# Feed-forward entry by column half, tile 0's weights split sooner, tile 1 in one region; a key chunk through another buffer; orders around keys and values

## The chip, the cores and the metric

The kernel runs on one core of a Trainium2 chip. The metric is the device time of one execution in microseconds (us), the median of several runs. All times inside the execution are from one profiled execution of the kernel before, counted from the start of its span.

## What is computed

A decoder trunk of two layers on 256 tokens of width 1024, all in float32:

```python
# layer 0: x += NSA(RMSNorm(x));      x += ConvGLU(RMSNorm(x))
# then:    k, v = RMSNorm_kv(x) @ kv_w                 # shared keys and values
# layer 1: x += DiffAttn(RMSNorm(x)); x += ConvGLU(RMSNorm(x))
# out = RMSNorm(x)
def conv_glu_ffn(h, w_in, conv_w, conv_b, w_out):
    u = h @ w_in                                       # 1024 -> 2 * 2752
    up = jnp.pad(u, ((0, 0), (CONV_WIDTH - 1, 0), (0, 0)))
    c = conv_b
    for tap in range(CONV_WIDTH):                      # 3 taps over the tokens
        c = c + up[:, tap:tap + S] * conv_w[tap]
    gate, val = c[..., :FFN_DIM], c[..., FFN_DIM:]
    return (jax.nn.silu(gate) * val) @ w_out
```

## The kernel before

Every float32 operand of a matmul is split into a high part (rounded, `..._hi`) and a low part (the rest, `..._lo`), and a product is three matmuls: high by high, high by low, low by high. The weights come in as chunks of 128 x 2048. SyncE loads a chunk into `stage` (two slots), ScalarE writes its high part into `win_hi` in two halves of 1024 columns, VectorE subtracts and writes `win_lo`, and TensorE uses both. SyncE issues loads in one fixed order, each after the wait that frees its slot; the code of each engine is likewise an order written out by hand, and an engine stands still until its next instruction's semaphores are there. Nothing is reordered between VectorE instructions or between ScalarE instructions.

The stages in order: six projection groups of the sparse attention (chunks 0 to 11; chunk 8 is the first half of the keys), compression and attention, the output projection (4 chunks, `C_WO`), the feed-forward of layer 0 (`ffn(0, ...)`), keys, values and queries of the differential attention (12 chunks from `C_KV`), its attention, its output projection (`C_DO`), `ffn(1, ...)`, the last norm.

A feed-forward runs over 22 tiles of 128 gate and 128 value columns. Tile j is `up(j)` on TensorE (into `psU`), then on VectorE and ScalarE a scaling by the row of 1/rms, a 3-tap convolution, SiLU, product and split (`act_hi`, `act_lo`), then `down(j)` on TensorE into `psA`. TensorE runs up(j+1) ahead of down(j). `up` uses one matmul over 512 columns (high weights by the high and low activations side by side) and one over 256; its two halves lie in two column regions of a bank, which ScalarE's copy (`u_part`) and a VectorE add bring together. Tile 0 is special: `up_raw` uses activations that are transposed unscaled while the norm is still being computed, and the scaling comes later through a row made by `row_T` and a VectorE copy (L1699).

Around the start of a feed-forward: `add_y` adds the projection to `x` in four pieces (token tile t, column half h) as TensorE finishes them; `raw_T` transposes a piece of x; `raw_hi` (ScalarE) and `raw_lo` (VectorE) write the transposed activations' parts; `square_halves`, `root_of`, `first_mean` and `newton_a` to `newton_d` make 1/rms; `split_in(j, b, h)` splits half h of the input weights of tile j, `split_out` the output weights of a tile. `step(j, b)` is one tile's work on ScalarE or VectorE.

## Time and profile before

| | |
|---|---|
| three runs | 663.27, 663.92, 664.14 us; median 663.92 |
| the profiled execution | 662.02 us, of which its span is 660.2 us |
| granted TensorE clock | 0.997 of full speed |
| TensorE matmuls (PE) busy | 632.3 us (96% of the span) |
| VectorE (DVE) busy | 535.2 us (81%) |
| ScalarE (ACT) busy | 417.7 us (63%) |

Busy shares are means over very different stages. In the timeline views below a row is: start in us, length in us, engine, line of the code, operation, output <- inputs, shapes, count; in brackets the idle time of the engine just before it and what ended it. Matmuls overlap in the pipeline, so a matmul's length is more than its spacing.

### The profile page before, as it was taken

The numbers are of one execution on the slowest core, as the hardware profiler recorded it, in microseconds if no ns is written. First come the engines' busy times: TensorE is split into PE (matmuls) and PEld (weight loads), VectorE is DVE, ScalarE is ACT, GpSimd is POOL, SyncE is SP. The second block draws the span as 40 slices with busy tenths as digits, with TensorE's granted clock in tenths as the row PEclk, the third lists the DMA queues.
The fourth block names the chain that finished last, engine by engine and source line by source line (L and its number), as shares of the span: only waits on it lengthen the run. The fifth ranks groups of instructions, "written<-read, shape, count | busy, mean of one in ns | idle before, by whom it ended". The sixth has DMA issues, their size and how long they took to land.

```text
span 660.2 us, 10782 instructions
## 1 busy us (share of the span) xinstructions
PE 632.3 (96%) x3614; PEld 527.9 (80%) x3614; DVE 535.2 (81%) x987; ACT 417.7 (63%) x815; POOL 25.2 (4%) x70
## 2 busy tenths in 40 slices
PE   8999989999999999999999999979999999999995
PEld 7998756678878888888888788757878888888894
DVE  4587598956998888888988547796899888888996
ACT  7554377827766666666667454673966666666665
POOL 2100000000000000000004000060000000000000
PEclk9999999999999999999999999999999999999998
DMA  8685030126455555545525545305455555555521
GB/s 287 239 283 210 5 123 2 66 72 248 159 196 213 195 190 187 198 186 191 186 77 192 189 147 184 120 1 216 169 178 215 189 189 186 189 190 184 191 105 65
DMA packets 21441, 109.12 MB, mean 165 GB/s; under 512 B 2592, under 2 KB 2976, under 8 KB 12448
## 3 DMA queue, kind: packets, MB, share of 16 engines
q1 hardware_dynamic: 21120, 108.48, 45.9%
q8 instruction: 19, 0.31, 0.2%
q10 hardware_dynamic: 288, 0.22, 0.1%
q14 instruction: 14, 0.11, 0.1%
HBM read 107.64 MB, written 1.05 MB: 165 GB/s over the span
## 4 chain that ended last, share of the span: by engine, by line
PE 76%; DVE 14%; ACT 4%; POOL 3%; issue 2%; DMA 1%; DVEq 0%; ACTq 0%; POOLq 0%
PE psU L545 19%; PE psA L406 12%; PE psA L408 12%; PE psA L407 12%; PE psU L550 10%; DVE win_lo L1531 2%; DVE stat L1803 2%; DVE win_lo L1445 2%; DVE arena L1832 1%; DVE arena L1559 1%; PE psU L758 1%; PE psU L743 1%; PE psU L525 1%; PE psU L524 1%; PE psU L523 1%
## 5 line engine op out<-in xcount | busy, mean ns | idle before, releaser
L545 PE MATMUL psU<-hA,win_hi 128*128 128x512 f32 x608 | 190.7, 395 | 1.0 <-DVE win_lo L1531 1.0
L550 PEld LDWEIGHTS psU<-hA,win_lo 128*128 128x128 f32 x608 | 114.2, 188 | 26.6
L550 PE MATMUL psU<-hA,win_lo 128*128 128x256 f32 x608 | 119.4, 278 | 0.0
L1531 DVE TENSOR_TENSOR win_lo<-stage,win_hi 128x1024 fp32r<-128x1024 f32 x89 | 108.6, 1222 | 5.7 <-ACT win_hi L1095 5.6
L1095 ACT ACTIVATE win_hi<-stage 128x1024 fp32r<-128x1024 f32 x92 | 96.0, 1050 | 9.1 <-PE psA L408 5.6
L545 PEld LDWEIGHTS psU<-hA,win_hi 128*128 128x128 f32 x608 | 95.3, 189 | 4.2 <-ACT win_hi L1095 1.4
L1445 DVE TENSOR_TENSOR win_lo<-stage,win_hi 128x1024 fp32r<-128x1024 f32 (+3 forms) x59 | 65.9, 1154 | 21.0 <-ACT win_hi L1032 20.7
L1559 DVE SCALAR_TENSOR_TENSOR arena<-arena,prm 128x255 f32<-128x255 f32 (+1 forms) x168 | 77.3, 481 | 3.7 <-ACT arena L1107 0.7
L406 PE MATMUL psA<-wout_hi,act_hi 128*128 128x512 f32 x176 | 69.3, 394 | 2.8 <-DVE act_lo L1598 2.2
L407 PE MATMUL psA<-wout_lo,act_hi 128*128 128x512 f32 x176 | 68.7, 390 | 0.0
L408 PE MATMUL psA<-wout_hi,act_lo 128*128 128x512 f32 x176 | 68.5, 389 | 0.0
L1032 ACT ACTIVATE win_hi<-stage 128x1024 fp32r<-128x1024 f32 (+3 forms) x56 | 53.5, 1002 | 21.6 <-PE psA L408 15.7
L1107 ACT ACTIVATE arena<-arena,prm 128x256 f32<-128x256 f32 x84 | 46.0, 595 | 26.0 <-DVE arena L1580 21.8
L406 PE MATMUL psA<-win_hi,hA 128*128 128x512 f32 (+3 forms) x160 | 60.3, 377 | 1.3 <-DVE win_lo L1445 0.8
L408 PE MATMUL psA<-win_hi,hA 128*128 128x512 f32 (+3 forms) x160 | 59.3, 371 | 0.0
L407 PE MATMUL psA<-win_lo,hA 128*128 128x512 f32 (+3 forms) x160 | 59.2, 370 | 0.0
L1549 DVE TENSOR_TENSOR wout_lo<-stage_out,wout_hi 128x1024 fp32r<-128x1024 f32 x42 | 51.3, 1222 | 0.0
L1116 ACT ACTIVATE arena<-psU 128x512 f32<-128x512 f32 x38 | 22.7, 598 | 44.3 <-PE psU L550 44.2
L1573 DVE TENSOR_TENSOR arena<-psU,arena 128x512 f32<-128x512 f32 x38 | 26.3, 692 | 22.5 <-ACT arena L1116 22.5
L1103 ACT ACTIVATE wout_hi<-stage_out 128x1024 fp32r<-128x1024 f32 x42 | 44.0, 1047 | 0.0
L1263 ACT ACTIVATE arena<-psA,stat 128x128 f32<-128x128 f32 (+1 forms) x88 | 35.9, 429 | 7.9 <-DVE stat L1803 7.6
L406 PEld LDWEIGHTS psA<-wout_hi,act_hi 128*128 128x128 f32 x176 | 33.0, 188 | 9.5 <-DVE act_lo L1598 2.6
(250 smaller groups left out, 1058.5 us busy)
## 6 DMA issues: line engine op xcount, KB each, us to landing
stage<-in_w_ffn_in SPq DMA_DIRECT2D x44, 1024.0 KB, 5.5
stage_out<-in_w_ffn_out SPq DMA_DIRECT2D x44, 516.0 KB, 3.5
stage<-in_w_kv SPq DMA_DIRECT2D x8, 1024.0 KB, 5.0
stage<-in_w_group SPq DMA_DIRECT2D x5, 1024.0 KB, 5.3
stage<-in_w_nsa_out SPq DMA_DIRECT2D x4, 1024.0 KB, 4.8
stage<-in_w_dq SPq DMA_DIRECT2D x4, 1024.0 KB, 4.9
stage<-in_w_dout SPq DMA_DIRECT2D x4, 1024.0 KB, 4.8
stage<-in_w_phi SPq DMA_DIRECT2D x2, 1024.0 KB, 4.8
```

Of the source, the lines that this page charges most:

```text
L406: mm(out, xh, wh, start=start, stop=False)
L407: mm(out, xh, wl, start=False, stop=False)
L408: return mm(out, xl, wh, start=False, stop=stop)
L545: mm(o, win_hi[:, slot, cs], hA[:, k, :, :].rearrange("p a q -> p (a q)"), start=k == 0, stop=False)
L550: last = mm(o[:, 0:S], win_lo[:, slot, cs], hA_hi[:, k2, :], start=False, stop=k2 == KT - 1)
L1032: act.activation(win_hi[:, s % 2, cs], stage[:, n % 2, cs], ACT.Copy).then_inc(sem["in_hi"], 1)
L1095: act.activation(win_hi[:, slot, h * W // 2:(h + 1) * W // 2], stage[:, slot, h * W // 2:(h + 1) * W // 2], ACT.Copy).then_inc(sem["in_hi" ...
L1107: act.activation(conv[:, b, g, :], src, ACT.Identity, bias=prm[:, b, 4 * g + 3:4 * g + 4], scale=prm[:, b, 4 * g + 2:4 * g + 3]).then_inc( ...
L1445: last = dve.tensor_tensor(win_lo[:, s % 2, cs], stage[:, n % 2, cs], win_hi[:, s % 2, cs].bitcast(F32), sub)
L1531: last = dve.tensor_tensor(win_lo[:, slot, cs], stage[:, slot, cs], win_hi[:, slot, cs].bitcast(F32), sub)
L1549: dve.tensor_tensor(wout_lo[:, b, :], stage_out[:, b, 0:D], wout_hi[:, b, :].bitcast(F32), sub).then_inc(sem["out_lo"], 1)
L1559: dve.scalar_tensor_tensor(conv[:, b, g, k:S], u_sum[:, g, 0:S - k], prm[:, b, 4 * g + 2 - k:4 * g + 3 - k], conv[:, b, g, k:S], ALU.mult, ...
```

## The change

It does the following.

- **Key chunk.** Chunk 8 is loaded into `keysT` (unused by then) right behind chunk 6, and not into `stage`; chunk 10 then waits only for chunk 6's slot, and some `phi` pieces are loaded at other places.
- **Feed-forward entry, by column half.** The last chunk of the output projection (`out_last`) now finishes column half 0 of both token tiles and then column half 1; `raw_T`, `add_y` and the squares follow that order, and only two column-half-1 transposes remain behind the projection.
- **Tile 0's weights.** Half 0 of tile 0's input weights is split into slot 1 of `wout_hi` and `wout_lo`, which needs no free slot of `win_hi`. `split_out(0, 0)` moves ahead of it on ScalarE and VectorE. `split_in(1, 1, 0)` moves forward between the activations' parts; the Newton steps come behind all of `raw_lo`.
- **Tile 1 in one region.** `up_second` uses three matmuls over 256 columns; ScalarE's `u_part` copy and VectorE's add fall away. On ScalarE both conv_first instructions now come ahead of `split_in(3, 1, 0)`; on both engines `split_in(3, 1, 1)` moves behind `act_hi` and `act_lo`.
- **Last tile.** ScalarE does SiLU, then the first half of the output weights, then `act_hi`, then the second half.
- **Keys and values.** `raw_T(2, 1, 0)` moves into `down_last`, `raw_T(2, 1, 1)` behind the first two k of the projection; VectorE adds piece (1, 1) behind the first two `h_lo`; the split of chunk `C_KV + 3` moves ahead of the wait for 1/rms.

```diff
+                if s != C_EARLY:
+                    load_main(s, a_groups[s // 2][s % 2], w4)
+                if s == C_EARLY - 2:
+                    sp.dma_start(keysT[:, :], a_groups[C_EARLY // 2][0]).then_inc(sem["keys_in"], 16)
                 if s == 2:
                     sp.dma_start(cols[:, O_PE:NCOL], a_cols[:, O_PE:NCOL]).then_inc(sem["params_in"], 16)
                     sp.dma_start(cmask[:, :], a_mask).then_inc(sem["mask_in"], 16)
-                if 3 <= s < 11:
-
-                    i = s - 3
+                for i in PHI_PIECES.get(s, ()):
...
+                            if half == 0:
+                                raw_T(2, 1, 1)
...
+                for n in range(2):
+                    for t in range(TT):
+                        if n == 1:
+                            raw_T(n_norm, t, 0)
+                        for k in range(2):
+                            last = out_three(h_hi, h_lo, slot, t, n, k, 6 + k)
+                        if n + t < 2:
+                            last.then_inc(sem["y_ready"], 1)
+                last.then_inc(sem["in_used"], 1)
+
+            def out_part(s0, h_hi, h_lo, h_waits, per_chunk, c, t, ks):
 
                 pe_.wait_ge(sem["oT_hi"], h_waits + per_chunk * (c + 1))
...
+                    pe_.wait_ge(sem["w0_half"], layer + 1)
                     for i, k in enumerate(T_ORDER):
+                        if i < 4:
+                            w_hi, w_lo = wout_hi[:, 1, :], wout_lo[:, 1, :]
+                        else:
+                            w_hi, w_lo = (w[:, slot, W // 2:W] for w in (win_hi, win_lo))
+                        if i == 4:
+                            pe_.wait_ge(sem["in_hi"], 2 * (first + 1))
+                            pe_.wait_ge(sem["in_lo"], first + 1)
                         if i == 2:
                             raw_T(n, 1, 1)
 
...
-                            last = up_pairs(g, 1, slot, range(kh * KT // 2, (kh + 1) * KT // 2))
+                            for k in range(kh * KT // 2, (kh + 1) * KT // 2):
+                                cs = slice(k * 2 * P + g * P, k * 2 * P + g * P + P)
+                                last = three_w((psT, psO)[g][:, 1, 0:S], slot, cs, k, k == 0, k == KT - 1)
...
                         if i == 2 and layer == 0:
                             raw_T(2, 0, 0)
+                            raw_T(2, 1, 0)
...
-                    split_in(j + 2, b, 1)
+                    if not late:
+                        split_in(j + 2, b, 1)
                     act.wait_ge(sem["prod"], j + (f0 + 1))
                     if not (isinstance(j, int) and j + f0 < 2):
 
                         act.wait_ge(sem["out_used"], j + (f0 - 1))
                     act.activation(act_hi[:, b, :], prod[:, b, :], ACT.Copy).then_inc(sem["a_hi"], 1)
+                    if late:
+                        split_in(j + 2, b, 1)
...
-                        act.activation(wout_hi[:, 1, cs], stage_out[:, 1, cs], ACT.Copy).then_inc(sem[done], 1)
-                    act.wait_ge(sem["gate2"], f0 + NJ)
-                    act.activation(silu[0:LAST, 1, :], conv[0:LAST, 1, 0, :], ACT.Silu).then_inc(sem["silu"], 1)
+                    act.activation(wout_hi[:, 1, HALVES[0]], stage_out[:, 1, HALVES[0]], ACT.Copy).then_inc(sem["last_hi"], 1)
                     act.wait_ge(sem["prod"], f0 + NJ)
                     act.activation(act_hi[0:LAST, 1, :], prod[0:LAST, 1, :], ACT.Copy).then_inc(sem["a_hi"], 1)
+                    act.activation(wout_hi[:, 1, HALVES[1]], stage_out[:, 1, HALVES[1]], ACT.Copy).then_inc(sem["out_hi"], 1)
...
+                split_out(0, 0, layer > 0)
                 split_in(0, 0, 0)
                 split_in(0, 0, 1)
-                split_out(0, 0, layer > 0)
                 inst, waits = (1, KT) if layer == 0 else (3, 4 * KT)
                 if layer == 0:
                     act.wait_ge(sem["eps_ready"], 1)
                 act.activation(warm, eps, ACT.Sqrt)
-                square_halves(n, 0)
-                root_of(n, 0)
+                for t in range(TT):
+                    square_half(n, t, 0)
                 raw_hi(layer, inst, waits, 0)
                 raw_hi(layer, inst, waits, 2)
-                square_halves(n, 1)
+                split_in(1, 1, 0)
+                square_half(n, 0, 1)
                 raw_hi(layer, inst, waits, 4)
-                root_of(n, 1)
+                square_half(n, 1, 1)
                 raw_hi(layer, inst, waits, 6)
-                split_in(1, 1, 0)
+                for t in range(TT):
+                    root_of(n, t)
                 split_in(1, 1, 1)
 
                 act.activation(warm, eps, ACT.Silu)
                 step(0, 0, halves=False)
-                step(1, 1)
+                step(1, 1, halves=False, late=True)
...
                 g = c // 2
                 if c == 1:
+                    split(C_KV + 3)
                     act.wait_ge(sem["rstd"], 2)
...
-                def step(j, b):
-                    add_and_scale(j, b)
+                def step(j, b, lo_first=False):
+                    if lo_first:
+                        times_row(j, psU[:, b, :, 0:S])
+                        take_params(j + 1, 1 - b)
+                    else:
+                        add_and_scale(j, b)
                     split_in(j + 2, b, 0)
                     taps(j, b)
                     product(j, b)
+                    if lo_first:
+                        product_lo(j, b)
                     split_in(j + 2, b, 1)
-                    product_lo(j, b)
+                    if not lo_first:
+                        product_lo(j, b)
                     split_out(j + 1, 1 - b)
...
+                take_params(0, 0)
+                split_out(0, 0)
                 split_in(0, 0, 0)
                 add_y(n, 0, 0, "in_used", first)
+                add_y(n, 1, 0, "in_used", first)
+                split_in(0, 0, 1)
                 add_y(n, 0, 1, "in_used", first)
-                split_in(0, 0, 1)
-                add_y(n, 1, 0, "in_used", first)
-                first_mean(n, 0)
-                add_y(n, 1, 1, "in_used", first)
+                for t in range(TT):
+                    first_mean(n, t)
                 raw_lo(0)
                 raw_lo(1)
+                add_y(n, 1, 1, "in_used", first)
                 raw_lo(2)
                 raw_lo(3)
-                first_mean(n, 1)
-                take_params(0, 0)
-                split_out(0, 0)
+                split_in(1, 1, 0)
                 raw_lo(4)
+                raw_lo(5)
+                raw_lo(6)
+                raw_lo(7)
                 newton_a()
-                raw_lo(5)
                 newton_b()
-                raw_lo(6)
                 newton_c()
-                raw_lo(7)
                 newton_d()
                 rows_of_rstd()
-                split_in(1, 1, 0)
...
-            for h in range(2):
-                for t in range(TT):
-                    add_y(2, t, h, "out_used", NJ)
+            add_y(2, 0, 0, "out_used", NJ)
+            add_y(2, 1, 0, "out_used", NJ)
+            add_y(2, 0, 1, "out_used", NJ)
             h_lo(hA_lo, hA_hi, O_KG, range(2))
+            add_y(2, 1, 1, "out_used", NJ)
             split(C_KV, (1,))
             h_lo(hA_lo, hA_hi, O_KG, range(2, KT))
```

Tile 1 on VectorE in a feed-forward, from its first instruction after `split_out(1, 1)` (`arena` holds the convolution's buffers; L1559 or L1618 are the taps, L1593 or L1652 the product). Before:

```order
L1573 TENSOR_TENSOR arena<-psU,arena 128x512 [waits u_part]
L1554 COPY prm<-stage_out 128x8 [waits stage_out0_full]
L1580 TENSOR_TENSOR arena<-arena 128x512 [waits u_sum]
L1531 TENSOR_TENSOR win_lo<-stage,win_hi 128x1024 [waits in_hi]
L1559 SCALAR_TENSOR_TENSOR arena<-arena,prm 128x255 [waits conv0]
L1559 SCALAR_TENSOR_TENSOR arena<-arena,prm 128x254 [waits gate1]
L1559 SCALAR_TENSOR_TENSOR arena<-arena,prm 128x255 [waits conv0]
L1559 SCALAR_TENSOR_TENSOR arena<-arena,prm 128x254 [waits val1]
L1593 TENSOR_TENSOR arena<-arena 128x256 [waits val2,silu]
L1531 TENSOR_TENSOR win_lo<-stage,win_hi 128x1024 [waits in_hi]
L1598 TENSOR_TENSOR act_lo<-arena,act_hi 128x256 [waits a_hi]
L1549 TENSOR_TENSOR wout_lo<-stage_out,wout_hi 128x1024 [waits out_hi]
```

and now:

```order
L1627 TENSOR_TENSOR arena<-psU,arena 128x512 [waits in_used]
L1613 COPY prm<-stage_out 128x8 [waits stage_out0_full]
L1590 TENSOR_TENSOR win_lo<-stage,win_hi 128x1024 [waits in_hi]
L1618 SCALAR_TENSOR_TENSOR arena<-arena,prm 128x255 [waits conv0]
L1618 SCALAR_TENSOR_TENSOR arena<-arena,prm 128x254 [waits gate1]
L1618 SCALAR_TENSOR_TENSOR arena<-arena,prm 128x255 [waits conv0]
L1618 SCALAR_TENSOR_TENSOR arena<-arena,prm 128x254 [waits val1]
L1652 TENSOR_TENSOR arena<-arena 128x256 [waits val2,silu]
L1657 TENSOR_TENSOR act_lo<-arena,act_hi 128x256 [waits a_hi]
L1590 TENSOR_TENSOR win_lo<-stage,win_hi 128x1024 [waits in_hi]
L1608 TENSOR_TENSOR wout_lo<-stage_out,wout_hi 128x1024 [waits out_hi]
```

The add and the wait for `u_part` are gone, and the second `win_lo` split stands behind `act_lo`. The first `win_lo` split stands where it stood, ahead of the taps.

The same tile on ScalarE, from `split_out(1, 1)` on (L1107 or L1157 are the two conv_first, L1124 or L1174 is SiLU). Before:

```order
L1103 ACTIVATE wout_hi<-stage_out 128x1024 [waits stage_out1_full]
L1116 ACTIVATE arena<-psU 128x512 [waits in_used,prod,conv_params]
L1095 ACTIVATE win_hi<-stage 128x1024 [waits in_used,stage1_full]
L1107 ACTIVATE arena<-arena,prm 128x256 [waits u_norm]
L1107 ACTIVATE arena<-arena,prm 128x256
L1124 ACTIVATE arena<-arena 128x256 [waits gate2]
L1095 ACTIVATE win_hi<-stage 128x1024
L1130 ACTIVATE act_hi<-arena 128x256 [waits prod]
L1103 ACTIVATE wout_hi<-stage_out 128x1024 [waits out_used,stage_out0_full]
```

and now:

```order
L1153 ACTIVATE wout_hi<-stage_out 128x1024 [waits stage_out1_full]
L1157 ACTIVATE arena<-arena,prm 128x256 [waits in_used,u_norm,prod,conv_params]
L1157 ACTIVATE arena<-arena,prm 128x256
L1145 ACTIVATE win_hi<-stage 128x1024 [waits in_used,stage1_full]
L1174 ACTIVATE arena<-arena 128x256 [waits gate2]
L1181 ACTIVATE act_hi<-arena 128x256 [waits prod]
L1145 ACTIVATE win_hi<-stage 128x1024
L1153 ACTIVATE wout_hi<-stage_out 128x1024 [waits out_used,stage_out0_full]
```

The copy from `psU` is gone, the first `win_hi` copy has moved from ahead of the two conv_first to behind them, and the second from ahead of `act_hi` to behind it.

TensorE at the end of layer 0's feed-forward and the start of keys and values (`psU<-ident,x` are the transposes of `raw_T`). Before:

```order
L417 MATMUL psU<-ident,x 128x128 [waits x_new]
L417 MATMUL psU<-ident,x 128x128 x3
L406 MATMUL psA<-wout_hi,act_hi 128x512
L407 MATMUL psA<-wout_lo,act_hi 128x512
L408 MATMUL psA<-wout_hi,act_lo 128x512
L417 MATMUL psU<-ident,x 128x128 [waits x_new]
L417 MATMUL psU<-ident,x 128x128 x3
L417 MATMUL psU<-ident,x 128x128 [waits x_new]
L417 MATMUL psU<-ident,x 128x128 x3
L417 MATMUL psU<-ident,x 128x128 [waits x_new]
L417 MATMUL psU<-ident,x 128x128 x3
L406 MATMUL psA<-win_hi,hA 128x512 [waits xT_hi,xT_lo,kv_half,in_hi]
```

and now:

```order
L430 MATMUL psU<-ident,x 128x128 [waits x_new]
L430 MATMUL psU<-ident,x 128x128 x3
L430 MATMUL psU<-ident,x 128x128 [waits x_new]
L430 MATMUL psU<-ident,x 128x128 x3
L419 MATMUL psA<-wout_hi,act_hi 128x512
L420 MATMUL psA<-wout_lo,act_hi 128x512
L421 MATMUL psA<-wout_hi,act_lo 128x512
L430 MATMUL psU<-ident,x 128x128 [waits x_new]
L430 MATMUL psU<-ident,x 128x128 x3
L419 MATMUL psA<-win_hi,hA 128x512 [waits xT_hi,xT_lo,kv_half,in_hi]
```

Two of the four pieces are transposed ahead of the last `down`, one behind it, and the fourth not before the projection's first two k.

## Rows read from the trace of the kernel before

**Rows 1.** Timeline of TensorE (PE): its waits, and starts named.

```profile
45.07 0.33 PE L408 MATMUL psA<-win_hi,hA 128*128 128x368 f32 x1
...
45.55 0.47 PE L406 MATMUL psA<-win_hi,hA 128*128 128x512 f32 x1
...
160.30 0.60 PE L417 MATMUL psU<-ident,x 128*128 128x128 f32 x4
...
161.34 0.36 PE L507 MATMUL psA<-hA,win_hi 128*128 128x256 f32 x1 [0.44 <-ACT hA L1072]
...
168.51 0.70 PE L545 MATMUL psU<-hA,win_hi 128*128 128x512 f32 x2 [0.51 <-DVE win_lo L1531]
...
183.73 0.50 PE L406 MATMUL psA<-wout_hi,act_hi 128*128 128x512 f32 x1 [1.10 <-DVE act_lo L1598]
...
192.15 0.40 PE L406 MATMUL psA<-wout_hi,act_hi 128*128 128x512 f32 x1
...
342.11 0.50 PE L406 MATMUL psA<-wout_hi,act_hi 128*128 128x512 f32 x1 [0.28 <-DVE act_lo L1668]
...
347.57 0.47 PE L406 MATMUL psA<-win_hi,hA 128*128 128x512 f32 x1 [0.32 <-DVE hA L1468]
...
364.74 0.47 PE L406 MATMUL psA<-win_hi,hA 128*128 128x512 f32 x1 [0.58 <-DVE win_lo L1445]
...
491.53 0.50 PE L406 MATMUL psA<-wout_hi,act_hi 128*128 128x512 f32 x1 [1.12 <-DVE act_lo L1598]
```

**Rows 2.** Timeline of VectorE (DVE), layer 0, tiles 0 to 2.

```profile
168.29 0.42 DVE L1699 COPY arena<-psA 128x256 f32<-128x256 f32 x1
...
177.22 0.69 DVE L1573 TENSOR_TENSOR arena<-psU,arena 128x512 f32<-128x512 f32 x1
...
178.55 1.22 DVE L1531 TENSOR_TENSOR win_lo<-stage,win_hi 128x1024 fp32r<-128x1024 f32 x1
...
181.70 0.43 DVE L1593 TENSOR_TENSOR arena<-arena 128x256 f32<-128x256 f32 x1
...
183.26 0.42 DVE L1598 TENSOR_TENSOR act_lo<-arena,act_hi 128x256 fp32r<-128x256 f32 x1
...
184.73 0.68 DVE L1573 TENSOR_TENSOR arena<-psU,arena 128x512 f32<-128x512 f32 x1
...
190.77 0.42 DVE L1598 TENSOR_TENSOR act_lo<-arena,act_hi 128x256 fp32r<-128x256 f32 x1
```

**Rows 3.** Timeline of ScalarE (ACT), layer 0, tiles 0 and 1.

```profile
168.07 1.28 ACT L1184 ACT_TABLE_LOAD   x1
...
178.67 1.10 ACT L1107 ACTIVATE arena<-arena,prm 128x256 f32<-128x256 f32 x2 [0.80 <-DVE arena L1580]
...
181.04 1.04 ACT L1095 ACTIVATE win_hi<-stage 128x1024 fp32r<-128x1024 f32 x1
...
182.16 0.42 ACT L1130 ACTIVATE act_hi<-arena 128x256 fp32r<-128x256 f32 x1
```

**Rows 4.** Timeline of SyncE's queue: issue of tile 0's output weights, both layers.

```profile
147.11 0.43 SPq L369 DMA_DIRECT2D stage_out<-in_w_ffn_out  x1
...
455.23 0.43 SPq L369 DMA_DIRECT2D stage_out<-in_w_ffn_out  x1
```

**Rows 5.** DMA issues of those two moments; last: us from issue to landing.

```profile
stage_out<-in_w_ffn_out SPq DMA_DIRECT2D x1, 516.0 KB, 5.7
...
stage_out<-in_w_ffn_out SPq DMA_DIRECT2D x1, 516.0 KB, 5.8
```

**Rows 6.** Timeline of ScalarE, last tile of layer 0 and keys' start.

```profile
339.21 1.16 ACT L1154 ACTIVATE wout_hi<-stage_out 128x512 fp32r<-128x512 f32 x2 [1.04 <-PE psA L408]
...
346.07 3.03 ACT L1042 ACTIVATE hA<-psU,cols 128x256 fp32r<-128x256 f32 x8 [0.70 <-PE psU L417]
```

**Rows 7.** Timeline of VectorE, keys and values.

```profile
346.94 0.88 DVE L1468 SCALAR_TENSOR_TENSOR hA<-psU,cols,hA 128x256 fp32r<-128x256 f32 x2 [0.40 <-ACT hA L1042]
...
351.21 2.35 DVE L1445 TENSOR_TENSOR win_lo<-stage,win_hi 128x1024 fp32r<-128x1024 f32 x2
```

More of the change, by code:

```diff
@@ L54, in sum_place @@
 def sum_place(n, t, h):
-    return 2 * h + t if n == 2 else 2 * t + h
+    return 2 * h + t if n in (1, 2, 3) else 2 * t + h
 T_ORDER = (0, 2, 1, 3, 4, 6, 5, 7)
@@ L612, in ffn @@
                 down(1, 1, False)
-                pe_.wait_ge(sem["u_sum"], sums(1))
+                pe_.wait_ge(sem["u_norm"], f0 + layer + 2)
                 up(3, 1)
@@ L1029, in split @@
                 for h in halves:
-                    act.wait_ge(stage_full[n % 2], 16 * (n // 2 + 1))
+                    if s == C_EARLY:
+                        act.wait_ge(sem["keys_in"], 16)
+                    else:
+                        act.wait_ge(stage_full[n % 2], 16 * loads_of(n))
                     cs = slice(h * w // 2, (h + 1) * w // 2)
-                    act.activation(win_hi[:, s % 2, cs], stage[:, n % 2, cs], ACT.Copy).then_inc(sem["in_hi"], 1)
+                    act.activation(win_hi[:, s % 2, cs], (keysT if s == C_EARLY else stage[:, n % 2, :])[:, cs], ACT.Copy).then_inc(sem["in_hi"], 1)
             def h_hi(dst, off, inst, lo_done=0, ks=range(KT)):
@@ L1091, in split_in @@
                     slot = (first + b) % 2
+                    if isinstance(j, int) and j == 0 and h == 0:
+                        act.wait_ge(stage_full[slot], 16 * loads_of(stage_of(first)))
+                        act.activation(wout_hi[:, 1, :], stage[:, slot, 0:W // 2], ACT.Copy).then_inc(sem["in_hi"], 1)
+                        return
+                    if isinstance(j, int) and j == 0:
+                        act.wait_ge(sem["in_used"], first - 1)
                     if h == 0:
-                        act.wait_ge(stage_full[slot], 8 * j + (16 * (stage_of(first + b) // 2 + 1) - 8 * b))
+                        act.wait_ge(stage_full[slot], 8 * j + (16 * loads_of(stage_of(first + b)) - 8 * b))
                         act.wait_ge(sem["in_used"], j + (first - 1))
@@ L1108, in conv_first, with step @@
                                    bias=prm[:, b, 4 * g + 3:4 * g + 4], scale=prm[:, b, 4 * g + 2:4 * g + 3]).then_inc(sem["conv0"], 1)
-                def step(j, b, halves=True):
+                def step(j, b, halves=True, late=False):
                     act.wait_ge(sem["conv_params"], j + (f0 + 1))
@@ L1378, in _ @@
                         exps(u, u, "d", free_diff, psU[:, u, :, :])
-                if c < 11:
+                if c < 11 and c != 1:
                     split(C_KV + c + 2)
@@ L1419, in _ @@
             for t in range(TT):
-                square_halves(4, t)
+                for h in range(2):
+                    square_half(4, t, h)
                 root_of(4, t)
@@ L1709, in ffn @@
                 split_out(1, 1)
-                step(1, 1)
+                step(1, 1, lo_first=True)
                 with dve.Fori(1, NJ // 2 - 1) as i:
@@ L1935, in _ @@
                 g = c // 2
+                if c == 1:
+                    split(C_KV + 3)
                 if c % 2:
```

86 lines of the change are left out of this document (48 added, 38 removed).

## The prediction

> **What bounds the kernel now.** I read the shares first (the table ahead of the rows): TensorE is busy 96% of the span, so only the places count where it stands still, and what stands behind them. The timeline of TensorE gives these [rows 1]. In layer 0: 0.44 us at 161.34 (`up_raw` waits for the first activation part), 0.51 at 168.51 (`up_second` waits for tile 1's low weights), 1.10 at 183.73 (`down(1, 1)` waits for `act_lo`), 0.28 at 342.11 (last tile), 0.32 at 347.57 and 0.58 at 364.74 (keys and values). The matmul at 45.55 starts 0.15 after the end of that at 45.07. A refill of the pipeline comes on top of each: a matmul of 512 columns follows another after 0.23 us although it is 0.39 long, so an idle time stands for 0.16 to 0.18 more; I add that. Layer 1 repeats layer 0 with a shift of 307.8 us (491.53 less 183.73). Everything that the change could win so is 0.33 + 0.45 x 2 + 0.76 + about 1, and 2 x 2.6 at the feed-forwards: some 8 us.
>
> The second look, at VectorE through tiles 0 to 2 [rows 2], decides how much of the 2.6 is to be had. From the row copy at 168.29 to the last `act_lo` at 190.77 VectorE has almost no pause. Tile 2's `act_lo` starts at 190.77 and TensorE can follow 0.47 later (as 183.26 is followed by 183.73 [rows 1, 2]), at 191.24; it really takes `down(2, 0)` at 192.15 [rows 1]. VectorE has thus only 0.91 us in hand there, and whatever TensorE wins before must fit into that or into time that VectorE wins.
>
> **Feed-forward, tile 1: VectorE's time.** Before, tile 1 takes VectorE from 177.22 to 184.73, 7.51 us [rows 2]. Now, with S as its start:
> - The multiply reads `psU` directly. ScalarE's first conv_first starts 0.73 behind it (before: 1.45 behind the add's start, the second of two such operations [rows 2, 3]). The two take 1.10, and only then comes ScalarE's copy of 1.04 for `split_in(3, 1, 0)` [rows 3]. VectorE's low half can start at S + 2.8 (pipelined starts overlap by some 0.1). Before it started at S + 1.33 (178.55) without a wait. The add that falls away saves 0.6 of VectorE's work, but VectorE now waits 2.1.
> - From this half to the product it is 3.15 (178.55 to 181.70) as before: product at S + 5.95. `act_hi` follows after 0.46 (181.70 to 182.16): S + 6.4. `act_lo` starts at S + 6.85.
> - ScalarE's copy of the upper half now starts behind `act_hi`, so VectorE's comes at S + 7.85, and with this half and `split_out`, 1.22 each less the overlap, tile 2 starts at S + 10.1. Before, all of it from `act_lo` on took 1.47 (183.26 to 184.73).
>
> Tile 1 costs VectorE 10.1 in place of 7.5: +2.6. Then tile 2 runs as before, 6.04 to its `act_lo` (184.73 to 190.77).
>
> **Feed-forward, ahead of tile 1.** The chain from the row copy to S is the same list of instructions, so S moves by as much as the row copy does. Replayed with the durations of these rows: the output projection ends at 160.30 [rows 1]; the chunk's column half 0 of token tile 0 is transposed 3.6 us earlier, at 156.7, if `add_y(0, 0)` is done. But VectorE now does `split_out(0, 0)` and half a weight split ahead of that add, and the output weights land only at 147.11 + 5.7 = 152.8 [rows 4, 5]. Copy on ScalarE, two VectorE splits of 1.14 and the add bring x to 156.9: 0.25 late, so the projection ends at 160.55. `up_raw` starts 0.35 later, not 1.04 later as before, takes 6.25 as before and ends at 167.15. Its Newton steps are done just before (last `raw_lo` at 165.6, then some 1.1). The row copy comes at 167.55 in place of 168.29: 0.75 earlier. In layer 1 the weights land at 455.23 + 5.8, which is 0.4 later against the rest; the gain there is 0.35.
>
> So `down(2, 0)` can start at 191.24 + 2.6 - 0.75 = 193.1 against 192.15: **layer 0 loses 0.9, layer 1 loses 1.3**. The waits of 0.44 and 0.51 go and that of 1.10 does too in name, but `down(1, 1)` waits some 2.2 (its `act_lo` at S + 6.85 with S = 176.5 is where it was, while TensorE is 1 us early), and `down(2, 0)` waits near 1. Tile 3 has room again (0.7 in hand), and from there on TensorE binds; nothing is given back. TensorE's own cost of one region is hidden there: 48 matmuls in place of 32, 0.1 us in all if 256 columns follow at 0.12; were it a full 1 us (a far bound), it would lie in the 2.2.
>
> A table load stands on this chain: ScalarE's load for SiLU at 168.07 takes 1.28 [rows 3]; in the new order it ends near 167.9, and tile 0's multiply is done at 168.6, so it is hidden. The Trainium skill (ScalarE: Activation LUTs, Rules for kernel authors) says to budget about 2.7 us for a switch to another table set. By that figure, as an estimate, the load would end 0.6 us after the multiply and each layer would lose 0.6 more. The trace's 1.28 decides; the case stands with the rival that the row comes later, and adds less than 0.05 to its chance.
>
> **Last tile (each layer).** ScalarE copies both halves of the output weights from 339.21 for 1.16 ahead of SiLU [rows 6]. Now SiLU goes first and its product is some 1.0 earlier; `act_lo` would be ready at 341.2, before TensorE gets there at 341.66. The wait at 342.11 goes: -0.45 in each layer (bounds 0 and -0.45).
>
> **Keys and values.** Two adds bring x to TensorE at 344.0 and 344.6; transposes and the last `down` end at 346.1. ScalarE's copies start 0.42 after the second transposes, VectorE's part 0.87 after that (346.07 to 346.94) and TensorE 0.63 later (347.57) [rows 1, 6, 7]: 346.55, 1.0 earlier. But the fourth transposes come 2.7 later, at 349.3, and cost their 0.46 there. ScalarE's copies 4 to 7 of 3.03 / 8 each wait for them, VectorE's behind these, and so the split of chunk `C_KV + 1`, at 351.21 before [rows 7], starts at 352.2; its half is there at 353.5. TensorE wants it at 352.5. The second half of group 0 starts at 353.5 against 347.57 + 5.44 = 353.0. So far +0.5 (with the last tile's 0.45 in it). The squares slip by 2.3 us and with them 1/rms, but the split of `C_KV + 3` no longer waits for it, so the 0.58 + 0.18 at 364.74 go. Together with the last tile of layer 0: **-0.3** (bounds +0.5, if the stall stays, and -1.2, if the fourth transposes are early enough).
>
> **Key chunk.** The start at 45.55 [rows 1] is behind a load; now the chunk is there early. **-0.3** (bounds: +0.4, if a megabyte in the queue makes chunk 7 late, which I find 0.5 us in time, and -0.33).
>
> **The sum**: +0.9 + 1.3 - 0.3 (last tile of layer 0, keys and values) - 0.45 (last tile of layer 1) - 0.3 = **+1.15 us**. The profiled execution is 662.02 with a span of 660.2; I expect 661.3 and 663.2. The median of before lies 1.9 above its profiled execution, so the same step gives 665.1.
>
> **Rivals.**
> - *The wait for ScalarE's split is not felt* (faster). If tile 1's lower half is ready when VectorE asks for it, tile 1 costs 7.5 - 0.6 + 1.1 = 8.0 and `down(2, 0)` starts as TensorE gets there, 2.0 and 1.6 earlier: -3.6 - 1.1 = -4.7, 659.2. For it: 2 us of waits vanish at sight. Against: the order puts both conv_first ahead of the copy. It decides from a wait of under 1 us there. Half-way cases give 661 to 663. Chance 0.2 together.
> - *The row comes later* (slower). Newton's steps now stand behind every activation part; if they end 0.8 late, they reach past the end of `up_raw` by 0.5 (they have 0.3 in hand) and each layer loses 0.5 more: 666.1. The same follows if the table load of 1.28 ends 1.3 later than I put it. Chance 0.2. The table switch by the Trainium skill's figure would act in this way and give 666.3.
> - *Keys and values stay as they are, or the key chunk makes chunk 7 late*: 1 us worse, 666. Chance 0.1.
> - The forecast, 663.9 to 665.9: chance 0.5.
>
> Under 0.2% (1.3 us) a measurement of this kernel tells nothing from no change. The forecast lies within it for the most part, its upper third and the two slow rivals beyond. Faster 0.2, same 0.42, slower 0.38. The range takes in all but the whole gain and the sum of all losses: 661.8 to 667.0.
>
> **What the new profile would show.** Right: VectorE idle about 2 us before `win_lo` L1590 in tile 1, released by ScalarE's L1145, and 0.6 more behind `act_lo`; TensorE waiting 2 us and more at `down(1, 1)` and near 1 at `down(2, 0)` for `act_lo`; no wait at the row, nor at the last tile; a new wait of 1 us in the first projection group for `C_KV + 1`. The prediction is wrong if `down(2, 0)` has no wait, or if `up_raw` ends after 168 against the same start.

## The result and the profile after

| | before | changed kernel |
|---|---|---|
| median of 15 runs each, on one chip | 662.93 us (662.22 to 664.79) | 665.98 us (664.33 to 668.57) |
| ratio | | 1.0045, 95% interval 1.0032 to 1.0058 |
| profiled execution | 662.02, span 660.2 | 664.87, span 663.1 |
| TensorE busy | 632.3 us | 634.3 us |
| VectorE, ScalarE busy | 535.2, 417.7 us | 534.6, 415.6 us |

The changed kernel is 0.45% slower, 3.0 us by the medians and 2.9 by the profiled executions. The forecast was 1.15 us slower, 665.1 us, with a range from 661.8 to 667.0.

The timeline of VectorE after, layer 0, tile 1 and the start of tile 2 (start us, duration us, engine, line, operation, tiles, shapes; in brackets the idle time before it and who ended it). It answers to [rows 2]:

```profile
176.69 0.68 DVE L1627 TENSOR_TENSOR arena<-psU,arena 128x512 f32<-128x512 f32 x1
177.29 0.17 DVE L1613 COPY prm<-stage_out 128x8 f32<-128x8 f32 x1
179.57 1.23 DVE L1590 TENSOR_TENSOR win_lo<-stage,win_hi 128x1024 fp32r<-128x1024 f32 x1 [2.12 <-ACT win_hi L1145]
180.71 1.91 DVE L1618 SCALAR_TENSOR_TENSOR arena<-arena,prm 128x255 f32<-128x255 f32 x4
182.73 0.43 DVE L1652 TENSOR_TENSOR arena<-arena 128x256 f32<-128x256 f32 x1
183.63 0.43 DVE L1657 TENSOR_TENSOR act_lo<-arena,act_hi 128x256 fp32r<-128x256 f32 x1 [0.48 <-ACT act_hi L1181]
184.58 1.23 DVE L1590 TENSOR_TENSOR win_lo<-stage,win_hi 128x1024 fp32r<-128x1024 f32 x1 [0.52 <-ACT win_hi L1145]
185.72 1.22 DVE L1608 TENSOR_TENSOR wout_lo<-stage_out,wout_hi 128x1024 fp32r<-128x1024 f32 x1
186.86 0.69 DVE L1632 TENSOR_TENSOR arena<-psU,arena 128x512 f32<-128x512 f32 x1
```

Tile 1 lasts from 176.69 to 186.86, 10.17 us against 7.51. The 2.12 at 179.57 is the wait for ScalarE's lower copy; on ScalarE that copy stands behind both first convolution steps:

```profile
177.49 1.09 ACT L1157 ACTIVATE arena<-arena,prm 128x256 f32<-128x256 f32 x2 [3.63 <-DVE prm L1613]
178.49 1.05 ACT L1145 ACTIVATE win_hi<-stage 128x1024 fp32r<-128x1024 f32 x1
```

ScalarE had nothing to do for 3.63 us ahead of those steps. The timeline of TensorE after, which answers to [rows 1]: `down(1, 1)` and `down(2, 0)` of layer 0, the keys and values, and the same two places in layer 1:

```profile
184.12 0.50 PE L419 MATMUL psA<-wout_hi,act_hi 128*128 128x512 f32 x1 [2.12 <-DVE act_lo L1657]
184.46 0.40 PE L420 MATMUL psA<-wout_lo,act_hi 128*128 128x512 f32 x1
...
193.37 0.50 PE L419 MATMUL psA<-wout_hi,act_hi 128*128 128x512 f32 x1 [0.64 <-DVE act_lo L1657]
...
347.89 0.47 PE L419 MATMUL psA<-win_hi,hA 128*128 128x512 f32 x1 [0.19 <-DVE hA L1524]
...
354.90 0.47 PE L419 MATMUL psA<-win_hi,hA 128*128 128x512 f32 x1 [0.84 <-issue]
...
493.36 0.78 PE L419 MATMUL psA<-wout_hi,act_hi 128*128 128x512 f32 x1 [2.12 <-DVE act_lo L1657]
493.93 0.63 PE L420 MATMUL psA<-wout_lo,act_hi 128*128 128x512 f32 x1
494.36 0.63 PE L421 MATMUL psA<-wout_hi,act_lo 128*128 128x512 f32 x1
...
503.36 0.40 PE L419 MATMUL psA<-wout_hi,act_hi 128*128 128x512 f32 x1
```

Both layers wait 2.12 us at `down(1, 1)`. In layer 0 the matmuls behind it go on as before (0.34 from the first to the second). In layer 1 they take 0.63 and follow each other after 0.43 instead of 0.23 us. The view by stretches shows why (PEclk is the third number from the end: the granted clock, 1.00 for 2.4 GHz and 0.50 for 1.2 GHz):

```profile
492.00:496.00 4.00, 2.64 (x6) 2.16 (x7) 3.00 (x4) 3.57 (x5) 0.00 (x0) 0.68 0.00 0
496.00:500.00 4.00, 4.00 (x20) 3.37 (x19) 3.93 (x9) 1.67 (x5) 0.00 (x0) 0.90 0.64 224
```

The clock was halved for 3.4 us behind that wait (0.32 and 0.10 of 4 us are missing, and half clock lacks half: 1.68 times 2). Before, this place shows 1.00 throughout.

The starts of like matmuls give the time section by section, in us (the profiled executions; "phi" is the first matmul with `phi_k`, "projection" the first matmul that reads `hB_hi`, "last down" the first matmul of the last `down` of the loop, "end of keys and values" the first matmul behind the sixteen transposes of `tokA`; the numbers are differences of such starts, so a line that only moved shows nothing):

| section | before | changed | change |
|---|---|---|---|
| start to first matmul of group 0 | 8.29 | 8.95 | +0.66 |
| to phi | 63.70 | 63.16 | -0.54 |
| to output projection | 59.13 | 59.11 | -0.02 |
| layer 0: projection to down(0, 0) | 43.04 | 42.20 | -0.84 |
| to down(1, 1) | 9.57 | 10.70 | +1.13 |
| to down(2, 0) | 8.42 | 9.25 | +0.83 |
| to last down | 144.05 | 144.20 | +0.15 |
| to the end of keys and values | 52.20 | 51.91 | -0.29 |
| to layer 1's projection | 54.83 | 54.86 | +0.03 |
| layer 1: projection to down(0, 0) | 38.73 | 38.33 | -0.40 |
| to down(1, 1) | 9.57 | 10.69 | +1.12 |
| to down(2, 0) | 8.42 | 10.00 | +1.58 |
| to the end | 160.3 | 159.7 | -0.5 |

### The profile page after: what moved, and what is told of

It is laid out like the page before. It is cut to its first block, busy times and chain, and to the rows that moved or that the text cites. A ratio compares the mean times of both kernels' runs of the same rounds, so it can differ in the third digit from the quotient of the medians.

```text
span 663.1 us, 10832 instructions
## 1 busy us (share of the span) xinstructions
PE 634.3 (96%) x3646; PEld 531.6 (80%) x3646; DVE 534.6 (81%) x985; ACT 415.6 (63%) x813; POOL 23.6 (4%) x70
## 4 chain that ended last, share of the span: by engine, by line
PE 75%; DVE 15%; ACT 3%; DMA 2%; issue 2%; POOL 2%; SPq 0%; DVEq 0%; ACTq 0%; POOLq 0%
PE psU L588 18%; PE psA L419 12%; PE psA L420 12%; PE psA L421 12%; PE psU L593 9%; DVE win_lo L1590 2%; DMA stage_out<-in_w_ffn_out 2%; DVE stat L1869 2%; DVE win_lo L1501 2%; DVE arena L1618 1%; DVE arena L1898 1%; PE psU L430 1%; PE psU L802 1%; PE psU L787 1%; DVE wout_lo L1608 1%
## 5 line engine op out<-in xcount | busy, mean ns | idle before, releaser
L588 PE MATMUL psU<-hA,win_hi 128*128 128x512 f32 x576 | 180.5, 395 | 0.0
L593 PEld LDWEIGHTS psU<-hA,win_lo 128*128 128x128 f32 x576 | 108.2, 188 | 25.2
L593 PE MATMUL psU<-hA,win_lo 128*128 128x256 f32 x576 | 113.1, 278 | 0.0
L1590 DVE TENSOR_TENSOR win_lo<-stage,win_hi 128x1024 fp32r<-128x1024 f32 x87 | 106.1, 1222 | 5.5 <-ACT win_hi L1145 5.5
L1145 ACT ACTIVATE win_hi<-stage 128x1024 fp32r<-128x1024 f32 x90 | 94.2, 1050 | 1.0 <-DMA stage<-in_w_ffn_in 1.0
L588 PEld LDWEIGHTS psU<-hA,win_hi 128*128 128x128 f32 x576 | 90.4, 189 | 2.8
L1501 DVE TENSOR_TENSOR win_lo<-stage,win_hi 128x1024 fp32r<-128x1024 f32 (+3 forms) x57 | 63.5, 1151 | 21.5 <-ACT win_hi L1077 21.4
L1618 DVE SCALAR_TENSOR_TENSOR arena<-arena,prm 128x255 f32<-128x255 f32 (+1 forms) x168 | 77.2, 480 | 3.7 <-ACT arena L1157 0.7
L1157 ACT ACTIVATE arena<-arena,prm 128x256 f32<-128x256 f32 x84 | 46.0, 595 | 33.8 <-DVE arena L1639 20.3
L1077 ACT ACTIVATE win_hi<-stage 128x1024 fp32r<-128x1024 f32 (+3 forms) x54 | 51.6, 1003 | 19.5 <-PE psA L421 15.8
L1632 DVE TENSOR_TENSOR arena<-psU,arena 128x512 f32<-128x512 f32 x36 | 24.9, 692 | 21.7 <-ACT arena L1166 21.7
L1174 ACT ACTIVATE arena<-arena 128x256 f32<-128x256 f32 x40 | 16.7, 418 | 38.7 <-DVE arena L1618 38.7
```

What stands on the lines that cost most here:

```text
L588: mm(o, win_hi[:, slot, cs], hA[:, k, :, :].rearrange("p a q -> p (a q)"), start=k == 0, stop=False)
L593: last = mm(o[:, 0:S], win_lo[:, slot, cs], hA_hi[:, k2, :], start=False, stop=k2 == KT - 1)
L1077: act.activation(win_hi[:, s % 2, cs], (keysT if s == C_EARLY else stage[:, n % 2, :])[:, cs], ACT.Copy).then_inc(sem["in_hi"], 1)
L1145: act.activation(win_hi[:, slot, h * W // 2:(h + 1) * W // 2], stage[:, slot, h * W // 2:(h + 1) * W // 2], ACT.Copy).then_inc(sem["in_hi" ...
L1157: act.activation(conv[:, b, g, :], src, ACT.Identity, bias=prm[:, b, 4 * g + 3:4 * g + 4], scale=prm[:, b, 4 * g + 2:4 * g + 3]).then_inc( ...
L1501: last = dve.tensor_tensor(win_lo[:, s % 2, cs], (keysT if s == C_EARLY else stage[:, n % 2, :])[:, cs], win_hi[:, s % 2, cs].bitcast(F32) ...
```

## The experiments

Runs e1 to e4 shared one chip (kernel before there: median 663.06), e5 to e8 another (662.69).

**e1: ScalarE's lower copy first.** In tile 1 the copy goes ahead of the wait for `u_norm`:

```diff
                     if halves:
                         act.activation(u_part, psU[:, b, :, S:2 * S], ACT.Copy).then_inc(sem["u_part"], 1)
-                        split_in(j + 2, b, 0)
+                    if halves or late:
                         split_in(j + 2, b, 0)
                     act.wait_ge(sem["u_norm"], j + (f0 + layer + 1))
                     for g in range(2):
                         conv_first(j, b, g, u_sum[:, g, :])
-                    if not halves:
+                    if not halves and not late:
                         split_in(j + 2, b, 0)
```

> The changed kernel, with one edit: in tile 1 ScalarE copies the lower half of tile 3's weights (split_in(3, 1, 0)) ahead of the two conv_first instead of behind them. My theory (the 2.1 us for which VectorE waits there set the time of both feed-forward heads): VectorE's wait of 2.12 us at 179.57 goes, down(1, 1) starts without a wait at 181.9 instead of 184.12, down(2, 0) near 191.2 instead of 193.37; in layer 1 the same 2.2 us, and with the wait of TensorE the stretch of half clock behind it, another 0.75. In all 4.5 to 5 us less than the changed kernel: a profiled execution near 660.0, 1.5 to 2 us faster than the kernel before. Rival (the chain is set by something else that is late next, so that the wait only moves): less than 1.5 us off the changed kernel, and a wait of 1 us or more still at down(1, 1).

Measured: median 660.52, ratio to before 0.9962 (0.9943 to 0.9982). The profiled execution took 662.74, not the 660.0 expected. Tile 1 in this kernel, ScalarE's lower copy and VectorE's timeline (3.1 us later as a whole, mainly because the clock was halved for 6.8 us at 98 to 106 us, in the attention):

```profile
178.32 1.07 ACT L1145 ACTIVATE win_hi<-stage 128x1024 fp32r<-128x1024 f32 x1 [1.35 <-DMA stage<-in_w_ffn_in]
179.79 0.69 DVE L1628 TENSOR_TENSOR arena<-psU,arena 128x512 f32<-128x512 f32 x1
180.39 0.16 DVE L1614 COPY prm<-stage_out 128x8 f32<-128x8 f32 x1
180.46 1.22 DVE L1591 TENSOR_TENSOR win_lo<-stage,win_hi 128x1024 fp32r<-128x1024 f32 x1
...
185.48 1.23 DVE L1591 TENSOR_TENSOR win_lo<-stage,win_hi 128x1024 fp32r<-128x1024 f32 x1 [0.53 <-ACT win_hi L1145]
```

ScalarE's copy itself waited 1.35 us for its load, and was done before VectorE needed it. The half follows without a wait, and TensorE goes from down(0, 0) to down(1, 1) in 8.47 us instead of 10.70, without a wait. To down(2, 0) it still takes 9.27, with a wait of 0.68:

```profile
185.00 0.50 PE L419 MATMUL psA<-wout_hi,act_hi 128*128 128x512 f32 x1
...
194.27 0.50 PE L419 MATMUL psA<-wout_hi,act_hi 128*128 128x512 f32 x1 [0.68 <-DVE act_lo L1658]
```

So one copy's place decides the sign of the whole change: from 0.45% slower to 0.4% faster. The rival (the wait only moves) is out: no wait is left at down(1, 1).

**e2: TensorE kept busy.** Ahead of `down(1, 1)`:

```diff
                 up(2, 0)
+                pe_.wait_ge(sem["u_norm"], f0 + layer + 2)
+                for k in range(8):
+                    mm(psT[:, 1, :], hA_hi[:, k % KT, 0:P], hA[:, k % KT, :, :].rearrange("p a q -> p (a q)"), start=True, stop=True)
                 down(1, 1, False)
```

> The changed kernel, with 8 more matmuls of 512 columns on TensorE ahead of down(1, 1) in each layer (1.85 us of work whose result nobody reads), so that TensorE waits 0.2 us there and not 2.1, and all else is where it was. My theory (a stretch of half clock follows when TensorE has stood still for 2.1 us, in some executions in one layer and in others in both, and this makes up 0.75 us and more of the loss and the wide spread of the changed kernel's times): no granted clock of 0.5 behind down(1, 1), the times lie close together near 664.2, 1 to 2 us under the changed kernel's median, although TensorE does more. Rival (the stretches of half clock come whatever TensorE did before): clock and spread as in the changed kernel, median the same or up to 0.3 us longer.

Measured: median 665.06, ratio 1.0033 (1.0018 to 1.0049). TensorE's wait is 0.26 and 0.29 us, and the clock stays at 1.00 behind it in both layers:

```profile
182.39 1.98 PE L658 MATMUL psU<-hA 128*128 128x512 f32 x8
184.63 0.50 PE L419 MATMUL psA<-wout_hi,act_hi 128*128 128x512 f32 x1 [0.26 <-DVE act_lo L1660]
...
491.51 1.98 PE L658 MATMUL psU<-hA 128*128 128x512 f32 x8
493.79 0.50 PE L419 MATMUL psA<-wout_hi,act_hi 128*128 128x512 f32 x1 [0.29 <-DVE act_lo L1660]
```

Layer 1 takes 9.26 to down(2, 0) as layer 0 does, not 10.00. Sixteen useless matmuls cost nothing, and where the clock stays at 1.00 layer 1 is 0.74 us shorter. That the matmuls kept the clock is not shown by this one profile: e7 below kept it in both layers with the wait in place, and takes 9.27 there. The mean granted clock of the twelve executions, 0.9936 against 0.9897, speaks for them. But the times do not lie close together (663.7 to 667.5), which I had expected them to, and by the median the gain is 0.9 us, with intervals that overlap. Other stretches of half clock remain (below).

**e3: tile 1 as before.** The two regions, `u_part`'s add and the orders of before in tile 1; the rest stays changed:

```diff
-                            for k in range(kh * KT // 2, (kh + 1) * KT // 2):
-                                cs = slice(k * 2 * P + g * P, k * 2 * P + g * P + P)
-                                last = three_w((psT, psO)[g][:, 1, 0:S], slot, cs, k, k == 0, k == KT - 1)
+                            last = up_pairs(g, 1, slot, range(kh * KT // 2, (kh + 1) * KT // 2))
...
-                step(1, 1, halves=False, late=True)
+                step(1, 1)
...
-                step(1, 1, lo_first=True)
+                step(1, 1)
```

> The changed kernel, with tile 1 as in the kernel before (two regions in PSUM, an added u_part, ScalarE's and VectorE's order of before in it); the column halves, the head's other orders, keys and values and the key chunk stay changed. My theory (tile 1 costs VectorE 2.6 us more, the rest of the head wins 0.35 to 0.75 in each layer): VectorE needs 7.5 us for tile 1, down(1, 1) starts at 183.2 (0.9 earlier than in the changed kernel) and down(2, 0) at 191.9, bound by TensorE (1.4 earlier); in layer 1 1.5 plus 0.75 of clock. The profiled execution near 661.3, within 1 us of the kernel before or up to 0.3% faster. Rival (the loss sits in the head's order ahead of tile 1): time as in the changed kernel, within 0.7.

Measured: median 662.65, ratio 0.9979 (0.9961 to 0.9998). From the projection to down(2, 0) it takes 60.56 us in layer 0 (before 61.03, changed 62.15). down(0, 0) comes 0.7 us sooner than before, down(1, 1) waits 1.20 for VectorE, down(2, 0) has no wait. The head's own orders win 0.5 us in layer 0 and 0.3 in layer 1; all that the change loses in the heads sits in tile 1.

**e4: keys and values as before.**

```diff
-                            if half == 0:
-                                raw_T(2, 1, 1)
...
-                            raw_T(2, 1, 0)
...
+            raw_T(2, 1, 0)
             raw_T(2, 0, 1)
+            raw_T(2, 1, 1)
...
-                    split(C_KV + 3)
...
-            add_y(2, 0, 0, "out_used", NJ)
-            add_y(2, 1, 0, "out_used", NJ)
-            add_y(2, 0, 1, "out_used", NJ)
+            for h in range(2):
+                for t in range(TT):
+                    add_y(2, t, h, "out_used", NJ)
             h_lo(hA_lo, hA_hi, O_KG, range(2))
-            add_y(2, 1, 1, "out_used", NJ)
...
-                if c == 1:
-                    split(C_KV + 3)
```

> The changed kernel, with all orders around keys and values as before (two transposes before the queries' set, add_y(2, 1, 1) ahead of the first lows, chunk C_KV + 3 split behind the norm); feed-forward and key chunk stay changed. My theory (the wait for chunk C_KV + 1, 0.83 us, takes the place of what was won): between 0.1 and 0.5 us more than the changed kernel. Rival (the new wait costs more than the edits win): 0.3 us or more less than the changed kernel. Both are near the limit of a timing, so the place of the matmuls at 365 against that at 340 decides: 24.7 us before the change.

Measured: median 665.76, ratio 1.0039 (1.0023 to 1.0055), no difference to the changed kernel by timing. Last down to the end of keys and values took 51.43 us, 0.48 less than in the changed kernel and 0.77 less than before. So the rival holds: the last tile's order wins, and the orders around keys and values lose half a microsecond. The new wait of 0.84 at 354.90 costs more than the shorter stall at 347.89 gives. The other profiles bear this out: with the changed orders this stretch takes 51.89 to 51.93 us in five of six (e7 apart, below), with those of before 51.43 here and 51.20 in e6. Of the 0.77, 0.49 is there when keys and values start (10.88 against 11.37 us behind the last down); the rest is a shorter wait further on, 0.31 at 366.27 in place of 0.58.

Here both layers show the halved clock behind `down(1, 1)`; the view by stretches of this kernel:

```profile
184.00:188.00 4.00, 3.59 (x9) 2.82 (x10) 3.48 (x6) 3.23 (x4) 0.00 (x0) 0.61 0.00 2
...
494.00:498.00 4.00, 3.99 (x12) 3.24 (x13) 3.52 (x5) 2.82 (x4) 0.00 (x0) 0.69 0.03 5
```

**e5: both copies early.** On top of e1, the upper half goes back between SiLU and `act_hi`:

```diff
-                    if not late:
-                        split_in(j + 2, b, 1)
+                    split_in(j + 2, b, 1)
                     act.wait_ge(sem["prod"], j + (f0 + 1))
...
-                    if late:
-                        split_in(j + 2, b, 1)
                     split_out(j + 1, 1 - b, not (isinstance(j, int) and j + 1 + f0 < 2))
```

> The changed kernel, with both of ScalarE's copies for tile 3 moved in tile 1: the lower half ahead of conv_first (as in e1) and the upper half between SiLU and act_hi, where it was before the change. Theory: in e1 TensorE still waits 0.68 and 0.63 us at down(2, 0), because VectorE stands 0.5 us behind act_lo for ScalarE's upper copy; that wait goes, and down(1, 1) to down(2, 0) takes 8.75 us instead of 9.26 in each layer: 1.0 us less than e1 between the first down of layer 0 and the end. Rival: ScalarE's copy delays act_hi, and down(1, 1) starts 0.3 us or more later, so that nothing is won.

Measured: median 659.65 of 6 runs, ratio 0.9946 (0.9926 to 0.9965); the interval overlaps that of e1, so the second copy's gain rests on the profiles. down(1, 1) to down(2, 0) takes 8.64 us in both layers, with no wait; `act_hi` was not later:

```profile
184.58 0.50 PE L419 MATMUL psA<-wout_hi,act_hi 128*128 128x512 f32 x1
...
193.22 0.50 PE L419 MATMUL psA<-wout_hi,act_hi 128*128 128x512 f32 x1
```

**e6: e5 and e4 together.**

> As e5, and all orders around keys and values as in the kernel before (as e4). Theory: the pieces add up. e4 took 51.4 us from the last tile's down to the end of keys and values where the changed kernel took 51.9 and the kernel before 52.2, so 0.5 us less than e5: in the stretches by sum about 659 us profiled where TensorE keeps its full clock, a median of 659.0 to 659.8, 0.5 to 0.6% faster than the kernel before. Rival (the orders of the last tile and of the next section hang together): no difference to e5 in that stretch.

Measured: median 659.23, ratio 0.9949 (0.9931 to 0.9968), profiled span 657.2. Last down to the end of keys and values took 51.20 against 51.89 in e5. By timing e5 and e6 can't be told apart; both are 0.5% faster than the kernel before. In layer 0 of this execution down(2, 0) waited 0.63 again, since ScalarE waited 2.00 us for tile 4's weights at 185.39.

**e7: the changed kernel again.**

> The changed kernel once more, word for word, beside the others on the same chip. So far a wait of 2.1 us of TensorE at down(1, 1) was followed by a stretch of half clock of 3.4 us in 3 of 4 layers (changed kernel and e4), and waits of 1.2 us and less there, or filled ones, in none of 8 layers. Theory: it shows in one layer or both here again, and the median is that of the changed kernel, 1.003 to 1.006 of the kernel before. Rival (chance): no such stretch in either layer. It also shows whether the first projection group starts late (8.95 us in the changed kernel's profile, 8.29 in that of before) by chance or by the change.

Measured: median 666.48, ratio 1.0048 (1.003 to 1.0066). The time is as the theory had it, the clock as the rival (chance) had it: neither layer shows a halved clock behind `down(1, 1)`, though both wait 2.1 us. In this execution a load came late at keys and values too (ScalarE waited 3.69 us for it, 1.19 in the first profile), and the wait that the change had removed was back; last down to the end of keys and values took 52.96 us:

```profile
367.59 0.47 PE L419 MATMUL psA<-win_hi,hA 128*128 128x512 f32 x1 [0.82 <-DVE win_lo L1501]
```

**e8: the key chunk alone.** `load_main` of chunk 8 is replaced by a load into `keysT` behind chunk 6, with the counts that follow from it, in the kernel before.

> The kernel before, with the key chunk's edit alone: chunk C_EARLY lands in keysT ahead of its turn, and the pieces of phi go behind other chunks. Theory: from the first projection group to phi's first matmul the changed kernel took 63.16 us and the kernel before 63.70; here 63.16 again, so 0.5 us faster than the kernel before, under what a timing tells apart. For the start, theory (chance): the first projection group starts between 8.3 and 9.6 us as in any kernel; rival (the change makes the start late): 8.3 here too, since nothing of the first 12 us differs from the changed kernel's, would rather point to chance as well; only a start above 8.8 in this kernel and 8.3 in the kernel before, each time, would speak for the key chunk's edit.

Measured: median 662.44, ratio 0.9995 (0.9984 to 1.0007): no difference. From group 0 to phi 63.17 us, as in the changed kernel. The start was at 8.73. The gap at 45.55 [rows 1] is gone, but the place is reached at 45.57. Whether the earlier landing would help an execution that starts early is not shown: e5, which started at 8.02, had a wait of 0.47 at 15.09 and was at the same place at 45.57 too.

## Why the prediction was right, and what it missed

- **The total: in the range, in part by luck.** The step was forecast as +1.15 and came as +3.0. That 665.1 lies so near 665.98 comes also from its base, 663.92, the median of three executions of the kernel before; fifteen give 662.93. From there the same step gives 664.1, and the range ends at 666.0. Two rivals name times as near, 666.1 (the row comes later) and 666 (keys and values stay as they are), but their mechanisms did not show: the row copy started at 167.74 against 167.55 forecast, and keys and values came as forecast in sum.
- **Tile 1's cost: right.** Forecast 10.1 us with a wait of 2.1 for the lower copy and 0.6 for the upper; measured 10.17, 2.12 and 0.52. e1 and e5 take the two waits away one by one, and 2.2 and 0.6 us of TensorE's time go with them.
- **Ahead of tile 1: right in size.** Forecast 0.75 and 0.35 earlier; to down(0, 0) it is 0.84 and 0.40 (e7 against e8, which both had half clock at the end of the attention before, give 0.35 in layer 1). The late `x` that the forecast had for layer 1 shows as a new wait of 0.52 at 466.25. The table load that the forecast spoke of took 1.28 us (166.51 to 167.79) and was over before the multiply at 168.20 ended, so it stayed hidden. The Trainium skill (ScalarE: Activation LUTs, Rules for kernel authors) budgets about 2.7 us for such a switch; the trace does not agree, since ScalarE's instruction before the load ends at 166.49 and the next starts at 167.80.
- **Layer 0: +1.12 against +0.9 forecast.** The waits were forecast as 2.2 and near 1 and came as 2.12 and 0.64.
- **Layer 1: +2.30 against +1.3.** Here a step failed: "an idle time stands for 0.16 to 0.18 more; I add that". A wait of TensorE was priced at its length and a refill, and all that follows at full clock. The clock fell to half for 3.4 us behind the wait. Twelve matmuls of `down(1, 1)` took 4.44 us (493.36 to 497.80) and not 2.89; the wait at down(2, 0), 0.64 and its refill in layer 0, took up half of these 1.55 us, and 0.76 was left (2.30 less the 1.54 of e2, which keeps the clock and is near the forecast). So layer 1 shows no wait at down(2, 0) at all, which the forecast had named as a sign that it is wrong; the time had gone into the slow matmuls ahead of it.
- **Last tile, keys and values: the sum right, the parts not.** Forecast -0.3 together, measured -0.29. But by e4 the last tile and what stays of the rest wins 0.77 and the orders around keys and values lose 0.48, where I had them at +0.15. The new wait came as forecast, 0.84 against 1.0. The old one at 364.74 went in one execution and came back in e7, because it hangs on a load. Layer 1's last tile won about 0.5 (forecast 0.45).
- **Key chunk: no gain that a timing shows.** Forecast -0.3; -0.54 by the section of the profile, but the first group started 0.66 later there, and from the start of the execution to phi it is +0.12. In e5, which has the edit and started at 8.02, the section took 63.89. In e8, alone, the median is 0.25 under that of before, and the interval (-0.16% to +0.07%) holds no change too.
- **The start: +0.66, most likely chance.** In nine profiles of kernels with the key chunk's edit, whose first 12 us are alike, the first matmul of group 0 starts between 8.02 and 9.57 us; the one profile of the kernel before, at 8.29, lies within that. One profile does not exclude a part of the change.

The 1.76 us between the forecast and the 2.91 of the sections are thus 0.76 of clock, 0.42 of start and key chunk together (+0.12 against -0.30), 0.46 in the heads apart from the clock (1.12 and 1.54 against 0.9 and 1.3), and 0.12 of small ones.

The granted clock also plays into the medians. Its mean over all runs is 0.990 in the three series whose kernels leave TensorE idle for 2.1 us (changed kernel 0.9897, e4 0.9894, e7 0.9897; 36 runs) and 0.9925 to 0.9952 in all others, 0.9925 in e5 with 6 runs (e1, e2, e3, e5, e6, e8, and the kernel before with 0.9946 and 0.9952). A difference of 0.003 to 0.005 of 665 us is 4 to 7 us at half clock, one or two stretches of 3.4 us in each execution.

Executions of like clock can be compared. With 0.995 and more, six of the changed kernel (this result and e7) have a median of 665.2, and 42 of the kernel before (two chips) 662.6: 2.7 apart. A straight line of time against clock through all 24 and all 61 gives 665.1 and 663.1 at 0.995: 2.0 apart. So, as an estimate, 2.0 to 2.7 of the 3.0 us stay at like clock, and 0.3 to 1.0 goes with the clock. e2's 0.9 by its median fits; none of this is an experiment on the clock alone.

What stays open: why a wait of 2.1 us was followed by the halved clock in 3 of 6 layers of the profiles only (none of 14 with a wait of 1.2 us or less there), and whether the matmuls of e2 or chance kept it.

## What to carry to other kernels

When an edit frees an engine of work but lets it wait for a copy on another, look at what that other engine does just before: here ScalarE stood idle for 3.6 us ahead of the steps behind which the copy had been put. Moving that one copy turned a loss of 0.45% into a gain of 0.4% (0.5% with both copies, which a timing does not tell apart). A copy moved ahead hangs on its load instead: in e1 it waited 1.35 us for it and still came in time. Price a wait of TensorE of some 2 us at more than its length, and read the granted clock behind it. And where an order of several engines is changed at three places, measure each alone: here the heads' order won, tile 1 lost, keys and values lost, and the sum hid it.

## What was new about the hardware

- Behind a wait of TensorE of 2.1 us in a stretch that is otherwise busy, the granted clock fell from 1.00 to 0.50 (2.4 to 1.2 GHz) for 3.4 us, in 3 of 6 cases. 512 columns then follow each other after 0.43 us instead of 0.23. With eight matmuls in the place of the wait the clock stayed at 1.00 in both layers of the one profile, and so it did in e7 without them; the mean granted clock was 0.9936 with them and 0.9897 without.
- Such stretches come elsewhere too, in some executions and not in others: in the sparse attention (6.8 us at half clock at 98 to 106 us in e1, e3 and e5) and at the end of the second attention (3.4 us at 439 to 446 us in e1, e4, e5, e7 and e8). The first lies behind a section in which TensorE is busy for 4.14 of 6 us. The kernel before is busy for 4.04 there, with the same waits of 1.09 and 0.87 us, and its clock stays at 1.00, so what decides is not shown; e1 by stretches:

```profile
92.00:98.00 6.00, 4.14 (x34) 2.57 (x32) 5.76 (x20) 5.71 (x24) 0.00 (x0) 1.00 0.00 0
98.00:106.00 8.00, 6.98 (x37) 4.62 (x38) 3.99 (x12) 3.38 (x13) 0.00 (x0) 0.57 0.01 3
```

  From phi to the output projection e1, e3 and e5 took 61.7 to 61.8 us and the seven others 59.1: this stretch alone costs 2.7 us, nearly as much as the whole change. It could explain the spread of the kernel before (661.6 to 666.8): of its 35 executions on the first chip, the 14 with a mean clock under 0.995 have a median of 664.3, the others 662.7. Its one profile has no such stretch, so that is not shown.
- The same load lands 2.5 us apart in two executions of one kernel: ScalarE's copy for a chunk of keys and values, which waits for it in both, starts 23.22 and 25.74 us behind the last down (at 360.79 and at 363.99, the changed kernel and e7). The start of the first group differs by up to 1.5 us between kernels whose code there is alike.
